# Parallel-branch decoder step with grouped MoE: another order of the closing LayerNorm, with tile 3's h rows added on GpSimd

## What is computed

```python
h = layer_norm(ALPHA * x + m, ln1_g, ln1_b)
f = moe_ffn(h, router_w, router_b, expert_w_gate, expert_w_up, expert_w_down)
y = layer_norm(ALPHA * h + f, ln2_g, ln2_b)
...
for e in range(N_EXPERTS):
    u = jax.nn.silu(t @ w_gate[e]) * (t @ w_up[e])
    out = out + gates[:, e:e + 1] * (u @ w_down[e])
```

## Time and profile before

| what | us |
|---|---|
| median of three runs | 1024.87 (1024.86 to 1025.07) |
| the profiled execution's own time | 1024.97 |
| its span, first to last instruction | 1023.1 |
| TensorE busy in the span | 998.7 (98%) |
| VectorE / ScalarE / GpSimd busy | 793.0 / 477.4 / 373.6 |
| mean granted TensorE clock | 0.992 of full speed |

### The profile page before, as it was taken

How to read it: one execution, slowest core, us unless ns; L and a number is a source line. 1 busy time by engine, 2 the same in 40 slices (tenths; PEclk the granted TensorE clock), 3 DMA queues, 4 the chain that set the end, 5 groups by cost and what they waited for, 6 DMA issues and landing times.

```text
span 1023.1 us, 19648 instructions
## 1 busy us (share of the span) xinstructions
PE 998.7 (98%) x7238; PEld 903.7 (88%) x7238; DVE 793.0 (78%) x981; ACT 477.4 (47%) x675; POOL 373.6 (37%) x288
## 2 busy tenths in 40 slices
PE   8999999999999999999999999997999999999996
PEld 7999999999999999999999999985677777777773
DVE  4698889888989996753444498237989899898997
ACT  4232322223232335234443233342878787888875
POOL 3344444444455655344544444420200000000264
PEclk9999999999999999999999999998999999999998
DMA  7432323323232222333224531737999999999854
GB/s 221 121 103 83 101 84 95 90 84 100 82 103 82 83 83 72 100 103 102 82 83 157 191 103 56 294 115 281 399 387 400 388 397 389 399 395 377 318 173 177
DMA packets 147290, 190.55 MB, mean 186 GB/s; under 512 B 6819, under 2 KB 114339, under 8 KB 147228
## 3 DMA queue, kind: packets, MB, share of 16 engines
q1 hardware_dynamic: 140107, 176.74, 49.7%
q0 software_dynamic: 3008, 10.55, 3.3%
q10 hardware_dynamic: 4129, 2.67, 1.0%
HBM read 179.16 MB, written 11.76 MB: 187 GB/s over the span
## 4 chain that ended last, share of the span: by engine, by line
PE 91%; DVE 4%; issue 2%; DMA 2%; ACT 1%; POOL 0%; ACTq 0%; SPq 0%; DVEq 0%; POOLq 0%
PE pr L1131 60%; PE pr L1324 16%; PE work L1324 8%; DMA sb_tok<-in_state_conv_b_dram 1%; PE work L1300 1%; PE work L1213 1%; PE work L1357 1%; PE pr L1365 1%; ACT ring L904 0%; DMA hs<-h_rows,ids 0%; PE work L1238 0%; PE work L1139 0%; PE work L1439 0%; PE pr L1289 0%; DVE w_down_lo L1776 0%
## 5 line engine op out<-in xcount | busy, mean ns | idle before, releaser
L608 POOL TENSOR_TENSOR w_lo<-raw,w_hi 128x512 fp32r<-128x512 f32 x208 | 296.9, 1447 | 326.5 <-ACT w_hi L760 326.5
L1131 PE MATMUL pr<-x_hi,w_hi 128*128 128x260 f32 x1264 | 255.2, 283 | 0.0
L1131 PE MATMUL pr<-x_hi,w_lo 128*128 128x260 f32 x1264 | 254.7, 283 | 0.0
L1131 PE MATMUL pr<-x_lo,w_hi 128*128 128x260 f32 x1264 | 254.3, 283 | 0.0
L764 ACT ACTIVATE ev<-pr 128x520 f32<-128x520 f32 x96 | 58.1, 605 | 372.9 <-PE pr L1131 372.9
L1131 PEld LDWEIGHTS pr<-x_hi,w_hi 128*128 128x128 f32 x1264 | 195.0, 188 | 0.3
L1131 PEld LDWEIGHTS pr<-x_hi,w_lo 128*128 128x128 f32 x1264 | 194.9, 188 | 0.0
L1131 PEld LDWEIGHTS pr<-x_lo,w_hi 128*128 128x128 f32 x1264 | 194.3, 188 | 0.0
L1593 DVE SCALAR_TENSOR_TENSOR work<-b_pad,par,work 128x512 f32<-128x512 f32 x224 | 148.1, 742 | 0.0
L760 ACT ACTIVATE w_hi<-raw 128x512 fp32r<-128x512 f32 x208 | 118.9, 623 | 2.8 <-DMA raw<-in_w_in_dram 2.3
L645 POOL DMA_INDIRECT hs<-h_rows,ids x15 | 19.3, 1287 | 247.4 <-DVE ids L1887 247.4
(11 more groups left out here) (408 smaller groups left out, 1737.5 us busy)
## 6 DMA issues: line engine op xcount, KB each, us to landing
raw<-in_w_in_dram SPq DMA_DIRECT2D x80, 512.0 KB, 3.7
w_gate<-in_expert_w_gate_dram SPq DMA_DIRECT2D x16, 2048.0 KB, 14.6
w_up<-in_expert_w_up_dram SPq DMA_DIRECT2D x16, 2048.0 KB, 13.5
w_down<-in_expert_w_down_dram SPq DMA_DIRECT2D x16, 2048.0 KB, 12.6
y_rows<-y_out SPq DMA_DIRECT2D x14, 384.0 KB, 12.3
raw<-in_w_a_out_dram SPq DMA_DIRECT2D x8, 512.0 KB, 3.9
raw<-in_w_c_out_dram SPq DMA_DIRECT2D x8, 512.0 KB, 4.0
raw<-in_w_b_out_dram SPq DMA_DIRECT2D x8, 512.0 KB, 4.1
```

Of the source, the lines that this page charges most:

```text
L608: pool.tensor_tensor(w_lo[:, slot, k], raw[:, slot, k], w_hi[:, slot, k].bitcast(F32), ALU.subtract).then_inc(w_split, 1)
L1131: mm = pe.matmul(pr[slot][:, h, 0:HALF], w[:, slot, k, :], x[:, k, h * HALF:(h + 1) * HALF], start=(k == 0 and w is w_hi and x is hi), sto ...
```

## The change

- GpSimd adds tile 3's h to its scaled pick, in SBUF, by one operation on 128x1024 values (columns of `y_a` taken with step 2), between the samples' first fetch and the branch. It counts in `const_ready`.
- TensorE's two products of h with the identity (four rows of the profile) are gone; `others(3)` waits for `const_ready` 8 in place of `end_act` 2 and `back_in`.
- VectorE's `partial(0)`, `partial(1)`, `partial(2)` each run one place earlier in the last expert, `others_first` runs ahead of the two `share_low`.
- In the LayerNorm, VectorE takes the samples' sum ahead of sum 3, and the samples' end ahead of `normalise(3)`, which is now last. Tile 2's upper half is scaled and shifted on VectorE (a new operation, 128x512, both inputs in SBUF), its lower half on ScalarE and GpSimd as before.
- ScalarE's order follows, and its table load moves to just behind the scaling of tile 3's pick. SyncE stores tile 2 in two halves, in the order tile 0, upper half of 2, tile 1, samples, lower half of 2.

```diff
@@ -551,11 +551,19 @@
             expert_pass(first, 0, 0)
 
             def results_out():
-                for b in range(3):
-                    sp.wait_ge(added, b + 1)
-                    sp.dma_start(y_prompt[0, b * P:(b + 1) * P, :], y_b[:, b, :]).then_inc(fin_out[0], 16)
-                sp.wait_ge(fin_ready, 3)
+                def rows_to(b, cols):
+                    sp.dma_start(y_prompt[0, b * P:(b + 1) * P, cols], y_b[:, b, cols]).then_inc(fin_out[0], 16)
+
+                sp.wait_ge(added, 1)
+                rows_to(0, slice(0, D))
+                sp.wait_ge(fin_ready, 1)
+                rows_to(2, slice(D // 2, D))
+                sp.wait_ge(added, 2)
+                rows_to(1, slice(0, D))
+                sp.wait_ge(fin_ready, 2)
                 sp.dma_start(y_sample[:, 0, :].rearrange("s (c f) -> (s c) f", f=CS), sy_a).then_inc(fin_out[0], 16)
+                sp.wait_ge(added, 3)
+                rows_to(2, slice(0, D // 2))
 
             n_max = further_passes(sp)
             with sp.If(n_max > C):
@@ -583,7 +591,7 @@
                 sp.nop()
             results_out()
 
-            sp.wait_ge(fin_out[0], 64)
+            sp.wait_ge(fin_out[0], 80)
             sp.wait_ge(fin_out[1], 32)
             sp.wait_ge(tails_out, 80)
             sp.wait_ge(states_out, 32)
@@ -723,10 +731,14 @@
             fetch(y_b, slot_ready, y_b_in, y_rows[0:(E - 1) * C, :])
             pool.wait_ge(end_dve, 2)
             fetch_samples(sy_a, 0, y_a_in, y_rows[0:EARLY * C, :])
+            pool.wait_ge(end_act, 2)
+            pool.wait_ge(back_in, 48)
+            pool.tensor_tensor(plain(y_a[:, 3, :]), plain(y_a[:, 3, :]), paired(h_back[:, 3, :]), ALU.add).then_inc(const_ready, 1)
             def add_rows():
                 for b in range(3):
                     pool.wait_ge(std2_ready, (5, 8, 11)[b])
-                    pool.tensor_tensor(y_b[:, b, :], y_a[:, b, :], ln2_rows[:, 1, :], ALU.add).then_inc(added, 1)
+                    cols = slice(0, D // 2 if b == 2 else D)
+                    pool.tensor_tensor(y_b[:, b, cols], y_a[:, b, cols], ln2_rows[:, 1, cols], ALU.add).then_inc(added, 1)
 
             n_max = further_passes(pool)
             with pool.If(n_max < C + 1):
@@ -947,6 +959,7 @@
                     act.wait_ge(slots_ready, 3)
                     act.wait_ge(y_a_in[3], 16)
                     act.activation(y_a[:, 3, :], y_a[:, 3, :], ACT.Copy, scale=s_wa[:, 3:4]).then_inc(end_act, 1)
+                    act.activation(r_tok[0:1, 0:1], eps_t[0:1, 0:1], ACT.Sqrt)
                     for h in range(2):
                         act.wait_ge(ps.done["down"], t * CH + CH + 2 * (h + 1))
                         act.activation(y_last_hi[:, half(h)], work[0][0:C, h, :], ACT.Copy, scale=last_gate[:]).then_inc(end_act, 1)
@@ -1035,32 +1048,32 @@
 
             def scaled(b):
                 act.wait_ge(var_ready, NORMED[b])
-                act.activation(y_a[:, b, :], y_a[:, b, :], ACT.Copy, scale=agg[:, b, 3:4]).then_inc(std2_ready, 1)
+                cols = slice(0, D // 2 if b == 2 else D)
+                act.activation(y_a[:, b, cols], y_a[:, b, cols], ACT.Copy, scale=agg[:, b, 3:4]).then_inc(std2_ready, 1)
 
             def normalised():
 
                 deviation(0)
                 deviation(1)
                 scaled(0)
-                deviation(2)
                 act.wait_ge(var_ready, NORMED[0])
                 act.activation(sz_in, sy_a, ACT.Copy).then_inc(end_act, 1)
+                deviation(2)
                 scaled(1)
-                deviation(3)
-                scaled(2)
                 act.wait_ge(end_mm, 7)
                 act.activation(s_agg[:, 1:2], pr[0][:, 0, 2 * CS:2 * CS + 1], ACT.Copy, scale=-1.0).then_inc(end_act, 1)
                 act.wait_ge(end_act, 6)
                 act.activation(sy_b, sz, ACT.Square, bias=s_agg[:, 1:2], accum_out=s_agg[:, 2:3]).then_inc(end_act, 1)
+                deviation(3)
                 act.wait_ge(end_mm, 8)
                 act.activation(s_agg[:, 3:4], pr[0][:, 0, 2 * CS + 2:2 * CS + 3], ACT.Sqrt, bias=eps_t[:, 1:2]).then_inc(end_act, 1)
+                scaled(2)
                 for h in range(2):
-                    act.wait_ge(fin_ready, 1 + h)
+                    act.wait_ge(fin_ready, 3 + h)
                     cols = slice(h * D // 2, (h + 1) * D // 2)
                     act.dma_start(y_prompt[0, 3 * P:4 * P, cols], y_a[:, 3, cols]).then_inc(fin_out[1], 16)
 
             def finish():
-                act.activation(r_tok[0:1, 0:1], eps_t[0:1, 0:1], ACT.Sqrt)
                 normalised()
 
             with act.If(n_max < C + 1):
@@ -1434,9 +1447,9 @@
 
             def share_last():
 
-                def others(b, begin=True):
+                def others(b):
                     for h in range(2):
-                        pe.matmul(z_tile[b][:, h, :], ident[:], y_a[:, b, h * D // 2:(h + 1) * D // 2], start=begin, stop=False)
+                        pe.matmul(z_tile[b][:, h, :], ident[:], y_a[:, b, h * D // 2:(h + 1) * D // 2], start=True, stop=False)
 
                 def own(b, h):
                     n = slice(b * P, (b + 1) * P)
@@ -1459,12 +1472,8 @@
                 own(2, 0)
                 own(2, 1).then_inc(end_mm, 1)
                 pe.wait_ge(first.half_ready, 3)
-                pe.wait_ge(back_in, 48)
-                by_pair = h_back[:, 3, :].rearrange("p (i g) -> p g i", i=2)
-                for h in range(2):
-                    pe.matmul(z_tile[3][:, h, :].rearrange("p (g i) -> p g i", i=2), ident[:], by_pair[:, h * D // 4:(h + 1) * D // 4, :], start=True, stop=False)
-                pe.wait_ge(end_act, 2)
-                others(3, False)
+                pe.wait_ge(const_ready, 8)
+                others(3)
                 own(3, 0)
                 own(3, 1).then_inc(end_mm, 1)
 
@@ -1939,6 +1948,8 @@
                         low_parts(ps, "up", s, t, slots="down")
                         if ps is first:
                             share_marks()
+                            dve.wait_ge(back_in, 48)
+                            partial(0, 16)
                         return
                     if m:
                         low_parts(ps, "up", s, t, (0, 1))
@@ -1976,19 +1987,17 @@
                 gated_part(ps, t, 0)
                 low_parts(ps, "down", 0, t, (1,), last=True)
                 if ps is first:
-                    dve.wait_ge(back_in, 48)
-                    partial(0, 16)
+                    partial(1, 16)
                 u_low_last(ps, t, 0)
                 gated_part(ps, t, 1)
                 low_parts(ps, "down", 0, t, (2, 3), last=True)
                 u_low_last(ps, t, 1)
                 if ps is first:
-                    partial(1, 16)
+                    partial(2, 16)
                     spread_samples()
-                    partial(2, 16)
+                    others_first()
                     share_low(0)
                     share_low(1)
-                    others_first()
 
             def find_slots():
                 do(dve.tensor_tensor(t2[:], oh1[:], e_off[:], ALU.mult))
@@ -2106,20 +2115,24 @@
                 normalise(0)
                 summed_up(2)
                 normalise(1)
-                summed_up(3)
-                normalise(2)
                 dve.wait_ge(y_b_in[4], 16)
                 dve.wait_ge(end_act, 5)
                 dve.wait_ge(partial_ready, NTB - 1)
                 do(dve.scalar_tensor_tensor(sz, sy_b, s_spread[:, 4:5], sz_in, ALU.mult, ALU.add, accum_out=s_agg[:, 0:1]), Tally(dve, end_dve, 4))
                 last[0] = chain
-                normalise(3)
+                summed_up(3)
+                normalise(2)
+                settle()
+                upper = slice(D // 2, D)
+                do(dve.scalar_tensor_tensor(y_b[:, 2, upper], y_a[:, 2, upper], agg[:, 2, 3:4], ln2_rows[:, 1, upper], ALU.mult, ALU.add), to_fin)
                 last[0] = chain
                 dve.wait_ge(end_act, 8)
                 do(dve.scalar_tensor_tensor(sz, sz, s_agg[:, 1:2], sln2[:, 0, :], ALU.add, ALU.mult))
                 do(dve.reciprocal(s_agg[:, 3:4], s_agg[:, 3:4]))
                 settle()
                 do(dve.scalar_tensor_tensor(sy_a, sz, s_agg[:, 3:4], sln2[:, 1, :], ALU.mult, ALU.add), to_fin)
+                last[0] = chain
+                normalise(3)
 
             dve.sem_inc(first.ids_ready, 1)
             dve.sem_inc(first.u_ready, 2)
```

## The result

| | time, us | span, us | clock |
|---|---|---|---|
| before, five runs | 1024.86 (1024.57 to 1025.07) | 1023.1 | 0.992 |
| the change, five runs | 1029.87 (1029.49 to 1031.56) | 1029.8 | 0.988 |

The change is slower: ratio 1.0054, 95% interval 1.0039 to 1.0069. The forecast was 1024.2, in a range of 1023.0 to 1025.7: no difference. The time lies above that range. The profiled execution is the slowest of the five, 1031.56.

A forecast was written before the change was run, and what follows sets the result against it. Bound: VectorE's and GpSimd's closing chains. Tile 0's sum starting at 1004.2, 15.4 to VectorE's last half, then its store's landing give span 1022.4, 0.7 off 1024.97, so 1024.3, median 1024.2; range 1023.0 to 1025.7.

The forecast's parts named there:

- What bounds the kernel now: Kernel's end: VectorE's and GpSimd's closing chains, almost equally long; samples' rows land last, at 1022.8; TensorE runs without a gap.
- The moved `partial`: Fills VectorE's 1.18 us gap free; GpSimd's row-number operations slow to one per product, slot_ready near 995.0 instead of 992.0.
- What sets S: Start of tile 0's sum: late first y_b fetch lands at 1000.6, delaying others_first, share_low, TensorE; 1004.2 instead of 1003.85.
- held once: First y_b fetch, started 995.1 to 995.3, is held by one w_down_lo and gets through at 997.2; chance 0.5.
- The rival of the late gather: First y_b fetch holds others_first, share_low, TensorE: held twice 1025.3, chance 0.18; next partial too 1026.7, thrice or more 0.06.
- VectorE's sum from S: From tile 0's sum to VectorE's last half: 15.06 us of operations, 15.4 with 0.3 added for a clash.
- the clash on the new half: Tile 2's new VectorE half meets GpSimd's add_rows of tile 1, both inputs in SBUF; 0.3 us added, between 0 and 0.4.
- No idle time ahead of tile 3's sum: On VectorE: without TensorE's h products tile 3 is ready 2.16 us earlier, removing the 0.66 us gap.
- GpSimd's addition of h: Takes 2.4 us near 1002.4; nothing waits up to 4.7. Slow-addition rival: 1026.6 at 7 us, chance 0.04.
- Table load: Moves into ScalarE's idle 1.41 us, pushes y_last_hi by 0.1, which delays nothing: 0.
- What the samples' store gives back: Kernel's end: a 2.5 us transfer lands last instead of the samples' 3.7 us one; gain 1.0 with tile 0's sum unchanged.

The follow-up runs named there:

- experiment 2: Kernel before with only VectorE's three partials moved one place earlier, others_first left behind both share_low: 1030.79 us, ratio 1.0058.
- experiment 3: Kernel before, VectorE untouched, GpSimd made to wait for the last w_down_lo ahead of the copies ending in slot_ready: 1030.62 us, ratio 1.0050.
- experiment 6: The change with 30 unused identity products on TensorE ahead of its wait for the samples' small product: 1028.58 us, ratio 1.0041 to the kernel before.
- experiment 4: Kernel before with only partial(0) moved into VectorE's 1.18 us gap, partial(1) and partial(2) where they were: 1026.25 us, ratio 1.0011.
- experiment 5: The change with two VectorE waits on its own preceding operation, ahead of partial(1) and between the last two w_down_lo: 1028.15 us, ratio 1.0023.
- experiment 7: The change with TensorE's small product for the samples behind the last down product, not ahead of it: 1030.74 us, ratio 1.0061.
- experiment 1: The change with VectorE's opening order as before; closing order and h on GpSimd kept: 1025.4 us, ratio 1.0002 to the kernel before.
- experiment 9: Kernel before with only tile 3's h rows moved from TensorE to one GpSimd addition: 1024.29 us, ratio 0.9989.
- experiment 8: As experiment 7, and both share_low ahead of others_first: 1029.02 us, ratio 1.0033 to the kernel before.
- experiment 10: As experiment 1, with tile 3's second half stored by SyncE, not ScalarE: 1024.42 us, ratio 0.9991 to the kernel before.
- experiment 11: As experiment 10, with VectorE taking a quarter of tile 2 in place of half: 1024.56 us, ratio 0.9991 to the kernel before.

## Why the prediction was wrong

*What bounds the kernel now.* The reading "TensorE runs without a gap there" was made from S on. Ahead of S, the prediction followed `slot_ready` only to the fetch of `y_b`. TensorE waits for it too, ahead of the last down product, and in the kernel before that wait had already been met, so it left no idle time in any row. Searching the code for every wait on that semaphore would have shown it. Experiments 2 and 3 show the cause, experiment 6 its two parts: 3.4 us of wait and up to 2.6 of clock behind it.

*The moved `partial`.* This is the step that failed: "next to VectorE's products with two SBUF inputs such a one takes 1.17 … one for each product … and `slot_ready` is done near 995.0". It was done at 998.6 (997.9 without the landmark's shift). "Costs VectorE nothing" is right for the gap, but the count of one small operation per product holds only where VectorE pauses between two of them (experiment 4). In the change the second `partial` follows a `w_down_lo` directly: where the next starts 0.08 before the end, the operation sits through both (experiment 5). Nor did the copy behind it slip into the free stretch ahead of the last two `w_down_lo`, on which the prediction's 995.0 rests: L719 started in it and took 2.74. That such products overlap could be read in the earlier trace rows: x2 with 2.35 us is less than twice 1.23.

*What sets S.* The fetch was not held once; it started 5.9 us later (999.43, less 0.69, against 992.81), and then took 1.10, alone. In experiment 7, where VectorE waits for it, its data are there at 1004.5 and not at 1000.6. The rival of the late gather had 1026.7 as its worst price. In the change nothing waited for the gather; experiment 7, where it does bound, took 1030.7.

*Right:* VectorE's sum from S. Last half at S + 15.20, against 15.4; the clash on the new half is 0.2 (0.95 against 0.75), not 0.3. No idle time ahead of tile 3's sum. GpSimd's addition of h took 2.43 in the change and 3.4 in experiments 1 and 9, and nothing waited for it there. Table load 0.

*What the samples' store gives back.* A term mis-sized. Forecast 1.0: a last landing of 2.5 plus 0.3. It took 3.0 to land and 1.1 from there to the span's end. The 0.3 was read behind SyncE's store, and ScalarE closes later behind its landing. S to the end: 19.3, not 18.2. So even with S as forecast, 1004.2, the span would have ended at 1023.5 against 1023.1 before; experiment 1, with S as before, shows no gain either.

## What to carry to other kernels

Before moving work into another engine's idle time, list who was using that idle time, and follow every waiter of what they produce, also those that never had to wait so far. A result that three engines need in turn costs its lateness through whichever door is open: mending one wait (experiment 7) changed only the place of the idle time. And an idle TensorE is dearer than its idle time, since the matmuls behind it may run at half the clock, as they did here.

## What the runs showed of the hardware that was not expected

- A GpSimd operation on 128x5 or even 8x1 values, 0.17 to 0.25 us alone, took 2.61 and 2.74 beside two VectorE products of 1.2 us, both inputs in SBUF, whose rows overlap by some 0.1, and ended behind the first of two where a break of 0.03 stood between them (experiment 5). It is caught even if its row starts 0.2 to 0.35 us ahead of the product (L719 in the change, L722 in experiment 5, L720 in experiment 7).
- After 3.6 us without a matmul the granted clock was 0.50 for 3 to 6 us of the matmuls behind (the change, experiments 2 and 3), and also for some 3 us after only 2.2 us without one (experiment 5); after 1.66 us it stayed at 1.00 (experiment 8), and so it did with 30 unused products in the place of the idle time (experiment 6).
- ScalarE's closing step came 0.4 to 1.1 us behind the landing of its last store (0.9 before, 0.8 after, 1.1 in experiment 10, but 0.5 in experiments 6, 8 and 11), SyncE's 0.1 to 0.2 behind its own (before, experiments 10 and 11). What sets it stays open.
